# Bidirectional RWKV-7 scan on one Trainium2 core: value and removal terms in one product, and the triangular solver's start on GpSimd

## The reference, cut to what matters

```python
def _rwkv_step(S, inp):
    r, w, kk, kka, kt, v = inp
    sk = einsum('bhij,bhj->bhi', S, kk)
    S = S * w[:, :, None, :] - sk[..., None] * kka[:, :, None, :] + v[..., None] * kt[:, :, None, :]
    return S, einsum('bhij,bhj->bhi', S, r)
...
    mu, var = mean(y), mean(square(y - mu))      # by head
    yn = (y - mu) * rsqrt(var + EPS) * ln_g + ln_b
    bonus = sum(sum(r * kt * r_k)) * v
    return ((yn + bonus) * g) @ w_o
```

## Time and profile before

| | us |
|---|---|
| median of 3 runs | 3841.06 (3841.0 to 3845.65) |
| the profiled execution, its own time | 3850.02 |
| its span | 3848.3 |
| TensorE busy, of the span | 3417.3 (89%) |
| VectorE busy | 1747.0 (45%) |
| ScalarE busy | 1178.4 (31%) |
| GpSimd busy | 552.4 (14%) |
| scan, first row on VectorE to the start of round 0's first state product | 1665.1 to 1703.2 |
| rounds 0 to 11 of the scan | 1703.2 to 2018.7 |
| mean granted clock of TensorE | 0.942 of full |

### The profile page before, as it was taken

How to read it: one execution, slowest core, us unless ns; L and a number is a source line. 1 busy time by engine, 2 the same in 40 slices (tenths; PEclk the granted TensorE clock), 3 DMA queues, 4 the chain that set the end, 5 groups by cost and what they waited for, 6 DMA issues and landing times.

```text
span 3848.3 us, 65362 instructions
## 1 busy us (share of the span) xinstructions
PE 3417.3 (89%) x28861; PEld 2311.7 (60%) x28861; DVE 1747.0 (45%) x2909; ACT 1178.4 (31%) x2057; POOL 552.4 (14%) x754
## 2 busy tenths in 40 slices
PE   6999989999999898745776899898989999989998
PEld 5777776343343766545664443236757888756887
DVE  4324641121222654963356222126855546855454
ACT  3225722111111565921112111003253234334233
POOL 2220120000000210048513000001102210101210
PEclk8999998999999998867888899999999999989999
DMA  6531147989886352987533999993203313212322
GB/s 246 184 107 52 61 167 266 375 313 370 317 313 262 124 182 98 313 223 183 145 102 133 344 415 420 419 420 133 88 22 118 113 62 107 70 54 99 101 86 77
DMA packets 314859, 739.32 MB, mean 192 GB/s; under 512 B 68248, under 2 KB 148896, under 8 KB 265424
## 3 DMA queue, kind: packets, MB, share of 16 engines
q1 hardware_dynamic: 302480, 697.18, 49.7%
q0 software_dynamic: 12096, 37.96, 3.1%
HBM read 673.19 MB, written 61.89 MB: 191 GB/s over the span
## 4 chain that ended last, share of the span: by engine, by line
PE 70%; DVE 10%; DMA 8%; ACT 5%; issue 2%; SPq 2%; POOL 0%; DVEq 0%; POOLq 0%; ACTq 0%
PE ps L62 66%; DMA raw<-in_moe_w_dram 6%; PE ps L66 4%; SPq L120 2%; DVE mx L75 1%; DVE mx L102 1%; DVE mrn L99 1%; DVE b L75 1%; DVE cr L75 1%; DMA Tb<-ot 1%; DVE o L75 1%; DVE o L81 0%; ACT cr L72 0%; DMA c<-in_w_ple_gate_dram 0%; ACT lw L72 0%
## 5 line engine op out<-in xcount | busy, mean ns | idle before, releaser
L62 PE MATMUL ps<-raw,xinT 128*64 128x512 f32 (+1 forms) x4096 | 591.6, 492 | 32.8 <-DMA raw<-in_moe_w_dram 23.6
L62 PEld LDWEIGHTS ps<-raw,xinT 128*64 128x64 f32 (+1 forms) x4096 | 196.0, 123 | 401.4 <-issue 288.1
L62 PE MATMUL ps<-wp,hp 128*128 128x512 f32 x1024 | 314.1, 393 | 8.6 <-ACT wp L72 8.6
L62 PE MATMUL ps<-cr,oTr 128*128 128x512 f32 (+2 forms) x1024 | 255.6, 382 | 3.5 <-ACT oTr L72 3.1
L75 DVE TENSOR_TENSOR mx<-mx,ps 128x512 f32<-128x512 f32 (+1 forms) x196 | 127.3, 663 | 234.6 <-PE ps L62 133.3
L62 PEld LDWEIGHTS ps<-wp,hp 128*128 128x128 f32 x1024 | 193.8, 190 | 49.0 <-issue 8.8
L62 PEld LDWEIGHTS ps<-cr,oTr 128*128 128x128 f32 x1024 | 187.6, 188 | 38.9 <-ACT oTr L72 3.6
L62 PE MATMUL ps<-wp,hTr 128*128 128x512 f32 x512 | 194.4, 389 | 0.0
L62 PE MATMUL ps<-raw,hidT 128*64 128x512 f32 x768 | 177.9, 602 | 3.2 <-DMA raw<-in_moe_w_dram 3.2
L62 PE MATMUL ps<-ar,naxh 128*128 128x512 f32 x576 | 147.4, 406 | 19.0 <-DVE ar L75 8.8
L75 DVE TENSOR_TENSOR wp<-c,wp 128x1536 fp32r<-128x1536 f32 x32 | 60.6, 1894 | 180.7 <-ACT wp L72 180.7
(11 more groups left out here) (535 smaller groups left out, 6332.4 us busy)
## 6 DMA issues: line engine op xcount, KB each, us to landing
raw<-in_moe_w_dram SPq DMA_DIRECT2D x384, 1024.0 KB, 7.7
c<-in_w_in_dram SPq DMA_DIRECT2D x28, 2048.0 KB, 9.3
mx<-in_ada_w_dram SPq DMA_DIRECT2D x14, 2048.0 KB, 8.0
raw<-in_ada_w_dram SPq DMA_DIRECT2D x8, 2048.0 KB, 13.5
a<-in_na_w_qkv_dram SPq DMA_DIRECT2D x6, 2048.0 KB, 7.9
c<-in_w_branch_dram SPq DMA_DIRECT2D x16, 512.0 KB, 5.9
c<-in_w_out_dram SPq DMA_DIRECT2D x4, 2048.0 KB, 10.8
c<-in_w_ple_gate_dram SPq DMA_DIRECT2D x4, 2048.0 KB, 7.9
```

The costliest lines, as they stand in the source:

```text
L62: return self.e.matmul(out, lhsT, rhs, start=start, stop=stop, skip_group_check=True) if self.e is not None else self
```

## The change

Cut to what the prediction speaks of. It does four things.

First, the layout: a chunk's values and its U now share one tile VU for each direction and chunk, V on the chunk's own half of the partitions (loaded straight from vd) and U on the opposite half; the features and the masks are laid out so that a product with k lands on the opposite half. The b and k products of `gram` come from one weight tile of 128 columns; x1 and x2 give X (columns of a) and the V and state part of y (columns of r) in one instruction, on opposite halves; v and s become one product over 128 partitions; y3 adds the U part into the same banks, which VectorE evacuates after each chunk, with tokens on partitions, so that 'mean' needs no transposes. x1 and y go in two turns, with a wait between them.

Second, the order: `rw_scan_order` is rewritten, and `const()` stands ahead of the 31 rows.

Third, the solver: the squares of blocks 0, 1 and 2 are loaded together ahead of everything; GpSimd's blocks have scratch of their own, and it stores the solved blocks and fetches the next squares on its own queue.

Fourth, the smaller ones: `Banks` hands out the bank that was released longest ago; main, own, bon, Q, X and scratch live in tiles that exist already; b, r, T and Tm are loaded in halves, each by a DMA of its own.

```diff
@@ -128,21 +128,23 @@
...
-        while self.next % 8 in self.held.values():
-            self.next += 1
-        b = self.next % 8
-        self.next += 1
+        b = next(x for x in self.queue if x not in self.held.values())
+        self.last(b)
...
     def release(self, key):
-        del self.held[key]
+        self.last(self.held.pop(key))
...
         if what == 'mean':
-            for half in range(2):
-                e.wait_ge(*P.pe.at('rw_y', c, half))
-                e.tensor_reduce(m[:, 8 * half:8 * half + 8], hv(P.bank('rw_y', c, half)), AX, ADD).then_inc(*P.dve.inc())
+            e.wait_ge(*P.dve.at('y', self.last(c), 1))
+            e.tensor_reduce(m, hv(y), AX, ADD).then_inc(*P.dve.inc())
             e.wait_ge(*P.dve.last())
             e.tensor_scalar(m, m, 1.0 / 64, None, MUL).then_inc(*P.dve.inc())
             e.wait_ge(*P.dve.last())
-            for half in range(2):
-                e.tensor_tensor(hv(y[:, 512 * half:512 * half + 512]), hv(P.bank('rw_y', c, half)),
-                                m[:, 8 * half:8 * half + 8].unsqueeze(2).to_broadcast([128, 8, 64]), SUB).then_inc(*P.dve.inc())
+            e.tensor_tensor(hv(y), hv(y), b16(m), SUB).then_inc(*P.dve.inc())
...
+    const()
     some(31)
-    const()
...
-        recur(r, 0, 'y1')
-        recur(r, 0, 'y2')
+        if more:
+            gram(r + 1, 0)
         one(r)
         recur(r, 0, 'u')
-        recur(r, 0, 'v')
-        if more:
-            gram(r + 1, 0)
-            gram(r + 1, 1)
+        recur(r, 1, 'x1')
         some(4 if r else 8)
         recur(r, 0, 's')
+        recur(r, 0, 'y')
         one(r)
-        recur(r, 0, 'y3')
-        recur(r, 1, 'x1')
         if more:
-            gram(r + 1, 2)
-            gram(r + 1, 3)
-            blocks(r + 1)
+            gram(r + 1, 1)
         some(3 if r else 8)
         one(r)
         recur(r, 1, 'x2')
-        recur(r, 1, 'y2')
         if more:
-            level(r + 1, 0)
+            gram(r + 1, 2)
+            blocks(r + 1)
         one(r)
         some(3 if r else 7)
         recur(r, 1, 'u')
-        recur(r, 1, 'v')
         if more:
-            level(r + 1, 1)
+            gram(r + 1, 3)
         recur(r, 1, 's')
-        recur(r, 1, 'y3')
+        recur(r, 1, 'y')
         some(3)
         one(r)
         if more:
+            level(r + 1, 0)
             recur(r + 1, 0, 'x1')
+            level(r + 1, 1)
         if r + 2 < 12:
             load_m(r + 2)
         if r in (2, 9):
...
             if what == 'x1':
                 banks = []
                 for p in range(2):
-                    b, free = P.banks.take(('x', r, i, p), (P.act, 'x', r, i), hold=True)
+                    b, free = P.banks.take(('x', r, i, p), (P.dve, 'y', r, i) if lat(r) else (P.act, 'x', r, i), hold=True)
...
+                e.wait_ge(*s_vu[r % 2].at('vu', r))
+                for turn in range(2):
+                    if turn:
+                        e.wait_ge(*P.pe.at('x1a', r, i))
+                    for k in range(4):
+                        for z in range(2):
+                            c, p = cut(z, i), z ^ turn
+                            h = 2 * k + p
+                            out = P.psum[:, banks[p], bank_of(z, k)] if lat(r) else P.psum[half(1 - c), banks[p], bank_of(z, k)]
+                            ins = e.matmul(out, G(r, z)[half(c), h, pair(c) if lat(r) else keys(c)], VU(r, z)[half(c), i, sh(h)],
+                                           k == 0 and (turn == 0 or not lat(r)), False)
+                    ins.then_inc(*P.pe.inc('x1' if turn else 'x1a', r, i))
...
                     for z in range(2):
                         for p in range(2):
-                            c = half(cut(z, i))
-                            ins = e.matmul(P.psum[c, banks[p], sh(k)], ar(r, z)[half(p), 0, k, c], state(r, z)[half(p), k, :], False, True)
+                            c = cut(z, i)
+                            out = P.psum[:, banks[p], bank_of(z, k)] if lat(r) else P.psum[half(1 - c), banks[p], bank_of(z, k)]
+                            ins = e.matmul(out, ar(r, z)[half(p), k, pair(c) if lat(r) else keys(c)], state(r, z)[half(p), k, :], False, True)
...
                 for z in range(2):
-                    b, free = P.banks.take(('s', r, i, z), (P.dve, 'sum', r, i, z), hold=True)
-                    banks.append(b)
-                    for f in free:
-                        e.wait_ge(*f)
-                for k in range(4):
-                    for z in range(2):
+                    e.wait_ge(*P.act.at('u', r, i, z))
+                    c = cut(z, i)
+                    for k in range(4):
                         for p in range(2):
-                            c, h = half(cut(z, i)), 2 * k + p
-                            ins = e.matmul(P.psum[half(p), banks[z], sh(k)], tm(r, z)[c, 0, sh(h)], V[c, chunk(r, z), hd(r, h)], k == 0, False)
-                ins.then_inc(*P.pe.inc())
-            if what == 's' and not last:
-                e.wait_ge(*P.act.at('u', r, i))
-                for k in range(4):
-                    for z in range(2):
-                        for p in range(2):
-                            c, h = half(cut(z, i)), 2 * k + p
-                            ins = e.matmul(P.psum[half(p), P.banks.place[('s', r, i, z)], sh(k)], tm(r, z)[c, 1, sh(h)], XU[c, 1, sh(h)], False, True)
+                            h = 2 * k + p
+                            ins = e.matmul(P.psum[half(p), b, bank_of(z, k)], tm(r, z)[:, c, sh(h)], VU(r, z)[:, i, sh(h)], (z, k) == (0, 0), True)
                 ins.then_inc(*P.pe.inc('s', r, i))
-                for z in range(2):
...
+            if what == 'y':
+                banks = [P.banks.place.get(('x', r, i, p), 0) for p in range(2)]
+                if lat(r):
+                    e.wait_ge(*P.act.at('u', r, i, 1))
+                    for turn in range(2):
+                        e.wait_ge(*(P.pe.at('ya', r, i) if turn else P.pe.at('x', r, i)))
+                        for k in range(4):
+                            for z in range(2):
+                                c, p = cut(z, i), z ^ turn
+                                h = 2 * k + p
+                                ins = e.matmul(P.psum[half(c), banks[p], bank_of(z, k)], G(r, z)[half(1 - c), h, reads(c)], VU(r, z)[half(1 - c), i, sh(h)],
+                                               False, True)
+                        ins.then_inc(*P.pe.inc('y' if turn else 'ya', r, i))
+                for p in range(2):
+                    P.banks.release(('x', r, i, p))
+                if i:
...
-                for p in range(2):
-                    e.activation(XU[:, 0, :].rearrange("p (k e i) -> p e k i", e=2, i=64)[:, p],
-                                 P.bank('x', r, i, p)[:, 0:256].rearrange("p (k i) -> p k i", i=64), ACT.Copy).then_inc(*P.act.inc())
+                for z in range(2):
+                    o = half(1 - cut(z, i))
+                    for p in range(2):
+                        e.activation(X[o].rearrange("p (k e i) -> p e k i", e=2, i=64)[:, p],
+                                     P.bank('x', r, i, p)[o, 256 * z:256 * z + 256].rearrange("p (k i) -> p k i", i=64), ACT.Copy).then_inc(*P.act.inc())
...
-                e.activation(XU[:, 1, :], P.bank('u', r, i), ACT.Copy).then_inc(*P.act.inc('u', r, i))
+                if r >= 2:
+                    e.wait_ge(*P.pe.at('recur', r - 2))
+                for z in range(2):
+                    o = half(1 - cut(z, i))
+                    e.activation(VU(r, z)[o, i, :], P.bank('u', r, i)[o], ACT.Copy).then_inc(*P.act.inc('u', r, i, z))
...
-                j, ks = 2 * step(r) + i, slice(4 * group(r), 4 * group(r) + 4)
-                e.tensor_tensor(St[:, :, ks, :], St[:, :, ks, :], emm[:, :, ks, j:j + 1].to_broadcast([128, 2, 4, 64]), MUL).then_inc(*P.dve.inc('state', r, i))
-            if what == 'y3' and i and lat(r):
-                e.wait_ge(*P.pe.at('y3', r, 1))
+                j = 2 * step(r) + i
                 for z in range(2):
-                    seen = step(r) >= 4
+                    a = (walk[0][j] if j != 3 else 7) if z == 0 else walk[1][j + 1]
+                    e.tensor_tensor(state(r, z), state(r, z), emm[:, z, ks, a:a + 1].to_broadcast([128, 4, 64]), MUL).then_inc(*P.dve.inc())
...
                 solve_row(e, P.pool, u)
+                if i == 31:
+                    e.wait_ge(*P.pool.last())
+                    for z in range(2):
+                        e.dma_start(Td[z][ORDER[z][n]].rearrange("h (d n) -> (h d) n", d=4), Tv_of(n)[64 * z:64 * z + 64]).then_inc(*s_td[n].inc())
+                    s_td[n].name('td', n)
+                    if n < 4:
+                        squares(e, n + 2)
...
-            if whole is not None:
-                e.wait_ge(*(P.pool if whole else P.dve).at('row', u - 1))
-                Tv = T_of(whole)
+            if whole == 0:
+                e.wait_ge(*P.dve.at('row', 30))
                 for z in range(2):
```

(29 more changed lines are left out.)

223 lines of the change are left out of this document (87 added, 136 removed).

## The result

The changed kernel takes 3893.99 us (median, 3891.25 to 3898.79) beside 3842.74 for the kernel before on the same chip: ratio 1.0134, 95% interval 1.0116 to 1.0151, so 51 us slower where 3813 was forecast. The profiled execution took 3896.0 (span 3894.0; before 3848.3), 45.7 us more.

| stretch, us | before | after | difference |
|---|---|---|---|
| first expert layer | 692.4 | 679.1 | -13.3 |
| its end to round 0 (features, solver's block 0) | 451.3 | 467.7 | +16.4 |
| rounds 0 to 3 | 103.1 | 114.7 | +11.6 |
| rounds 4 to 9 | 166.8 | 163.8 | -3.0 |
| round 10 | 31.0 | 31.9 | +0.9 |

The account below looks back on a forecast made before the run. It took the scan's chain of hand-overs between TensorE, VectorE and ScalarE, with stops and lowered clock, as the bound, no engine being full. +11 - 11 - 21.6 - 4 - 2 = -27.6 gave 3813 us from 3841.1; range 3785 to 3846.

Parts of the forecast that it names:

- the change touches only the scan and the read-out: Scope of the forecast: only the scan and the read-out change, some 370 us of a span of 3848.3.
- Ahead of round 0: Start of the scan, before round 0: later row start +4, engines colliding +8, shorter way to the turned load -1; +11 us.
- The meeting of the two engines: VectorE's 62 row instructions beside GpSimd's: 0.13 us more each, 8 us, bounds 0 and 20; full collision +12, chance 0.14.
- From the rows' end to the turned load about 9: Ahead of round 0: from the end of VectorE's rows to the turned load about 9 us, where before had 9.9.
- Rounds 0 to 3: First four scan rounds: GpSimd's blocks earlier, then SP's queue sets round 4's start; 92 us instead of 103.1, -11.
- Latent rounds: Scan rounds 4 to 9: fewer matmul records, fewer stops, less clock loss; 24.2 us a round instead of 27.8, -21.6 in all.
- The stops for "issue": TensorE's stops in a latent round fall from 3.0 to 0.8 us; rival that stops and clock stay: 3831, chance 0.15.
- The drains: Latent rounds: some 13 tiling-mode changes a round, by the skill's rule 2 to 4 us a round; not in the sum.
- hidden, narrowly: Latent rounds: the turned load lands 17.5 us after the last round's end and is needed after 18, so costs nothing.
- My clock term: Latent rounds: the loss from TensorE's lowered clock falls from 2.6 to 1.8 us a round, since TensorE pauses less.
- SP's queue: Rival: SP's 28 issues a latent round become the bound, from about 0.65 us an issue on; +37, 3850, chance 0.13.
- Round 10 and the read-out: End of the scan: the means lose eight transposes a chunk; -4 in round 10, -2 in the read-out, 0 in round 11.

Follow-up runs that it names:

- turned_ahead_only: The changed kernel with one pair swapped in SP's order, the four turned loads ahead of the twelve of F: 3853.04 us, ratio 1.0011 to the kernel before.
- turned_first: The changed kernel, SP's order alone: turned loads first, then V and Tm, w_o and V, F last: 3863.07 us, ratio 1.0041 to the kernel before.
- sum_a: turned_ahead_only with the start of the scan and the two merges' bank rotation as in the kernel before: 3824.82 us, ratio 0.9939 to the kernel before.

## Why the prediction was wrong

For the scan and the read-out -27.6 us was forecast, and some +34.6 found (ahead of round 0, rounds 0 to 3, 4 to 9, 10 and 11, and the read-out); the merges and the expert layer add 13.5.

**What bounds the kernel.** The step that failed first is the sentence "the change touches only the scan and the read-out". It was in the diff: a class that all stages use. The price was 26.8 us in the merges and some -13 in the expert layer (9 of them shown as the banks' on the average of the profiles), neither in the sum nor a rival.

**Ahead of round 0**: +11 forecast, +16.4 found. The meeting of the two engines was 12.2 us (24.35 to 36.54) where I took 8 between bounds of 0 and 20; without GpSimd the rows take 23.36, so it is 13.2 in all. My reason, short instructions and GpSimd's pauses, was too hopeful: the median instruction went from 375 to 613 ns. The page's rule that I weighed there, an exclusive lock (the Trainium skill, SBUF — State Buffer, Who interferes with whom), gave the 20 us bound; the measured 0.20 to 0.21 an instruction lies between, and GpSimd paid nothing (38.3 us for its block beside the rows, 38.7 without them), so the rows show one side waiting and not both. "From the rows' end to the turned load about 9": 10.1 (1693.20 to 1703.28), then 3.4 to round 0; before 9.9 and 3.9. The later start was as forecast (+4): 7.3 us from the fence to the first row, where before had 4.0.

**Rounds 0 to 3**: -11 forecast, +11.6 found. GpSimd's blocks were early as expected, but the transposes before round 2 still waited, 9.42 us, for the turned load in SP's queue, and 24.23 before round 4:

```profile
1748.05 0.77 DVE L69 STREAM_TRANSPOSE mx<-mx 128x256 f32<-128x256 f32 x2 [9.42 <-DMA mx<-Td]
```

I had asked when GpSimd's block would be done and not when SP would come to its load. With the turned load ahead of F these rounds took 92.5, against my 92, but the parts were not mine: the first three took 57.8 where I had 52.5, the fourth 34.7 where I had 40. The total is in part luck.

**Latent rounds**: -21.6 forecast, -3.0 found, and -23.2 with one pair of SP's issues swapped. Laid end to end I had 21.1 us at full clock; rounds of 21.7 to 22.0 stand in five kernels. The 64x128 products took 1.90 (1.8 forecast), X 1.32 (1.53), U 1.21 (1.2). The stops for "issue", forecast to go from 3.0 to 0.8 a round, went from 26.5 to 0.5 us over six rounds (4.4 to 0.1 a round; my 3.0 was read from one round). The drains that would eat the gain (the Trainium skill, TensorEngine Tiling (Array Packing), Key Properties), priced at 2 to 4 us a round, were not seen: the chain of `turned_ahead_only` leaves 1.7% for everything between instructions, and its round takes 21.7 us where mine, laid end to end without them, has 21.1. What failed is "hidden, narrowly": I timed the turned load at 17.5 us and its need at 18, and both were off. In round 7 of the changed kernel it was issued 14.2 to 17.8 us after the round's start and had landed at 19.6. In a round that waits for nothing (`turned_first`, round 6, start 1859.95) VectorE comes to the transposes 14.3 us after the start:

```profile
1874.20 0.76 DVE L69 STREAM_TRANSPOSE mx<-mx 128x256 f32<-128x256 f32 x2
```

That is the need, since the fourth mask stands behind them in VectorE's order (`blocks` now ahead of `gram(r + 1, 3)`), and x1 and the levels behind the mask. In `turned_ahead_only` it is issued 5.3 us after the start. The change of VectorE's order was in the diff and I costed it at nothing, against my own rule to ask what is queued behind a wait. My clock term (2.6 to 1.8 us a round) had the wrong sign: behind each wait the clock was low, and its mean went from 0.90 to 0.84.

**SP's queue** was the rival with 0.13, priced +37 and 3850, "from about 0.65 an issue on". That condition was met: the 28 issues of a latent round took 19.5 to 21.4 us, 0.70 to 0.76 each, where I had forecast "some 17 us". A single one took 0.51 to 0.60, but some of each round took 1 to 2 us. The path was the rival's own, and so, nearly, was its price: 27.3 us a latent round (it had 28.3) and rounds 0 to 3 23 us over the forecast (it had 12). Two of its sums, which change nothing, are off: 26.2 with 0.8 of stops and 1.8 of clock is 28.8 and not 28.3, and the range's lower end adds up to 3789 and not 3785.

**Round 10 and the read-out**: -6 forecast, +0.9 and about +1 found, and +7.7 in round 11, where I said 0: its 96 records of x1, s and reads run at 1.2 GHz (7.54 us, where 96 such records take 4.73 in round 7) and the means wait for the last read. 18.7 became 23.6 to 27.8 in every kernel with the new products. That cause is read from the trace, no run isolates it.

## What to carry to other kernels

Look in a diff first for what the changed stage shares with others (an allocator, a ring, a semaphore order), and cut the whole span of both traces at common landmarks before explaining any stage. When transfers are cut smaller, count the issues ahead of each load and ask which engine's order stands behind the one that is last. A wait that ends well inside a round can cost its length again and more through the clock, so the few microseconds of a queue decide whether a leaner product shows at all.

## What was not expected of the hardware

- A transfer's price on SP hardly depended on its bytes: 0.60 us for half of a Tm transfer (64 partitions), 0.43 for the whole one (128), and in the changed kernel 0.51 as a rule for an F transfer, whole or by chunk. Some took 1 to 2 us, and one behind 4 MB 9.68.
- GpSimd and VectorE side by side slowed VectorE's instructions by 0.2 us each and GpSimd's not at all (38.3 us for a block beside VectorE's rows, 38.7 without).
- Five rounds whose stops were all under 0.5 us ran at 2.4 GHz throughout (`sum_a`; 0.94 over the six). With waits of 5 us every second round the mean was 0.84. And a round with two stops of 1.02 and 0.71 us ran at 1.2 GHz from 1885 to 1898 (`turned_first`, round 7), though TensorE was busy 12.15 of these 13 us.
